# Combination and norm by tiles in one program, the attention half of the output projection first, a third modulation group in the preparation

## The chip, the cores and the metric

One Trainium2 chip; the kernel uses one core of it. The metric is the device time of one execution in microseconds (us). The engines are TensorE (PE; its weight loads are shown apart as PEld), VectorE (DVE), ScalarE (ACT), GpSimd (POOL) and SyncE (SP). Each runs its own stream of instructions in order and waits on semaphores. SP, ACT and POOL also issue the DMA transfers.

## The reference

The trunk of a diffusion backbone: 1024 latent and 256 context tokens of width 1024, two layers, everything in fp32.

```python
for layer in range(2):
    # six rows per condition: shift1, scale1, gate1, shift2, scale2, gate2
    mods = silu(cond) @ mod_w[layer] + mod_b[layer]      # cond: c (latent), c_ctx (context)
    h = rms_norm(x) * (1 + scale1) + shift1
    if layer == 0:                                       # [attention | RWKV-7] side by side
        u = h @ w_in
        a = gqa_attend(...)                              # 512 columns
        v, kk, w, k, r = rwkv_prepare(token_shift(u))    # sigmoids, exps, per-head norm of k
        y = delta_scan(forward) + delta_scan(backward)   # 512 columns
        y = group_norm(y) * gn_w + gn_b + sum(r * k * r_k) * v
        out = concat([a, y * g]) @ w_out                 # g = sigmoid(glr) @ g2
    else:
        out = differential_attention(h) @ w_out
    x = x + gate1 * out
    h = rms_norm(x) * (1 + scale2) + shift2
    gates, expert_id = top-1 group, then top-2 experts in it
    x = x + gate2 * sum_k gates[k] * expert_mlp(h)[k]    # 32 experts, sorted into blocks of rows
return rms_norm(x_latent) * final_gain
```

## The kernel before

The tokens are cut into ten tiles of 128 rows (`NT`); the first two (`CT`) are context. `build` (L3570) runs the phases one after another, each a block with one stream per engine, and a phase starts when the one before is complete on all engines. In the order of the first layer: modulation's first group (`mods_phase`), `norm_phase`, input projection, attention, `rwkv_shared_phase` (L1192), `rwkv_prep_phase` (L1296, "the preparation"), the scan, `readout_outproj_phase` (L2369, "the readout"), `route_phase` (L2958), `experts_phase`, `combine_phase` (L3444), and then the second layer's `norm_phase` ("n1"), which reads from DRAM what `combine_phase` wrote there.

**Modulation.** The product silu(cond) @ mod_w is cut into six groups of 2048 columns over both layers, each written as (layer, group). A group needs eight loads of 1 MB (`Mods.load`, on SP) into a ring of `MRING` = 4 slots, eight products of four matmuls each (`Mods.product`, L122), and one addition of the bias on DVE (`Mods.add`, L130). Load n waits until product n - 4 has been done. Two groups are in the shared and preparation phases ((0,2) and (1,0)) and two in the first layer's route phase ((1,1) and (1,2)); the results go to DRAM at the end of the phase. Groups of layer 1 are read by the second layer's phases.

**Preparation.** SP's stream loads the input rows, the small columns of the first head pair and the identity, then two modulation loads, then 52 small constants of the scan (`const.load_constants`, L1266 to L1282), then ten more modulation loads. ACT copies the transposed values (`vt`), squares the keys (`sq`), takes the roots of the head norms, then the sigmoids and exponentials of the decay. DVE multiplies and adds over 128 x 1281 elements from the normed key up to `key1` (L1475), adds the modulation groups, and makes `ksum`, `rk0` and `rk`. PE does modulation products 3 and 4, the transposes `vt`, product 5, the head norms `n0` to `n2`, the low-rank products, products 6 to 15, and last the ten `srk` matmuls (L1401), which wait for `rk`. The scan starts when this is done.

**Readout.** Rounds m of two row tiles u. DVE's `read(m)` centres and norms y (L2629 is its first instruction, a sum over each head), POOL makes the bonus and the weighing and copies the gate operand `gs` (L2486), PE makes the gates (`bankG`, L2522), and DVE multiplies them to `yo`. `yo` is written to DRAM beside the attention's half and read back as one row `o` of 1024. PE turns `o` (L2532), ACT copies the turned tile to fp32r (`oh`, the lead) and DVE subtracts it from the original (`ol`, the rest); the weights are split in the same way into `wh` (ACT, L2600) and `wl` (DVE, L2674), out of a ring of two loads. `products` (L2543) are 24 matmuls for each half of 512 columns: lead times lead, lead times rest and rest times lead for eight rows k. `RowNorm` (L2247) norms the result tile, turns it and computes the router's logits (L2361). In the stream of every engine, round 0, the weights and round 1 stand ahead of the loop over tiles.

**Route.** PE does four modulation products (loads with a ring of 4) before the matmul that ranks the tokens, two and four between the steps, and the rest after the matmuls that make the list of slots; DVE copies the list (L3240) and adds the two groups. The stage ends when the groups are in DRAM.

**Combination.** Pairs of tiles: POOL gathers the two experts' rows of each token (indirect DMAs), DVE scales and adds them, multiplies with gate2 (L3528) and adds x; ACT stores the result (L3559). After that n1 loads it again, norms it and turns it into the resident `hT` (lead and rest), which the second layer's projection (first load at L695) reads.

## Time and profile before

| | |
|---|---|
| timed runs | 4481.32, 4473.69, 4473.89 us; median 4473.89 |
| the profiled execution's own time | 4474.47 us |
| its span in the trace | 4472.7 us |
| mean granted clock of PE (share of full speed) | 0.917 |
| busy PE / PEld | 3745.6 us (84%) / 2428.8 us (54%) |
| busy DVE / ACT / POOL | 1867.3 (42%) / 1373.7 (31%) / 576.5 us (13%) |

The shares are means over many phases. In the trace the preparation lies between 744.78 and 848.91 us, the scan up to about 1606, the readout between 1606.19 and 1839.82, the route phase up to 1911.84, and combination and n1 together between 2601.20 and 2725.17. The granted clock is given as a share of 2.4 GHz: 0.50 is 1.2 GHz.

In rows of the timeline the first number is the start in us from the span's start, the second the time in us to the end of the group; then engine (SPq and ACTq are the queues' own instructions), line, operation, output <- inputs, shape, and how many instructions stand together. Brackets give the idle time before it and what ended it.

### The profile page before, as it was taken

How to read it: one execution, taken by the hardware profiler on the slowest of the kernel's cores; microseconds unless marked ns; L12 is line 12 of the kernel's file. 1: busy time of each engine (PE TensorE's matmuls, PEld its weight loads, DVE VectorE, ACT ScalarE, POOL GpSimd, SP SyncE). 2: the span in 40 equal slices, each digit the busy share in tenths (PEclk: the TensorE clock that was granted, in tenths of full speed). 3: DMA queues.
4: the chain of work that ended last, by engine and by line, in shares of the span. 5: the costliest groups of instructions: out<-in, count | busy, mean ns of one | idle time of the engine just before them, and what ended most of it. 6: DMA issues, size and time to landing. Idle time of an engine off the chain costs nothing. (4 is left out here: it accounts for less than half of the span.)

```text
span 4472.7 us, 88140 instructions
## 1 busy us (share of the span) xinstructions
PE 3745.6 (84%) x34494; PEld 2428.8 (54%) x34495; DVE 1867.3 (42%) x4520; ACT 1373.7 (31%) x3101; POOL 576.5 (13%) x898
## 2 busy tenths in 40 slices
PE   3998996698988959679999926998999795999992
PEld 1886553488888837423333305896666582333331
DVE  3322554677777656400000045424777653000004
ACT  2211564366666322011111102113666520111111
POOL 0000000034444323000000020100000010000001
PEclk6999998799999979689999967999999896999996
DMA  6221002422222244489997883214000234899984
GB/s 247 71 86 73 10 10 79 151 60 79 68 78 73 58 133 156 166 350 364 389 375 311 323 312 108 86 65 156 10 11 10 89 123 181 340 360 400 412 355 178
DMA packets 250474, 772.07 MB, mean 173 GB/s; under 512 B 76624, under 2 KB 164688, under 8 KB 219056
## 3 DMA queue, kind: packets, MB, share of 16 engines
q1 hardware_dynamic: 200624, 646.00, 38.6%
q10 hardware_dynamic: 36144, 72.89, 4.3%
q0 software_dynamic: 13392, 48.76, 2.8%
q8 instruction: 225, 3.69, 0.4%
q14 instruction: 89, 0.73, 0.1%
HBM read 642.16 MB, written 117.54 MB: 170 GB/s over the span
## 5 line engine op out<-in xcount | busy, mean ns | idle before, releaser
L3372 PE MATMUL ex_bY<-ex_w,ex_aT 128*64 x880 | 390.8, 597 | 51.0 <-DVE ex_aT L3437 46.2
L3372 PE MATMUL ex_bG<-ex_w,ex_xT 128*64 x880 | 392.3, 599 | 17.3 <-DMA ex_w<-in_moe_w_gate 17.3
L3372 PE MATMUL ex_bU<-ex_w,ex_xT 128*64 x880 | 390.5, 597 | 7.6 <-DMA ex_w<-in_moe_w_up 7.6
L3373 PE MATMUL ex_bG<-ex_w,ex_xT 128*64 128x512 f32 x880 | 392.3, 599 | 0.0
L3373 PE MATMUL ex_bY<-ex_w,ex_aT 128*64 128x512 f32 x880 | 391.1, 597 | 0.0
L3373 PE MATMUL ex_bU<-ex_w,ex_xT 128*64 128x512 f32 x880 | 390.5, 597 | 0.0
L3435 DVE TENSOR_TENSOR ex_a<-ex_sg,ex_bU 128x512 f32<-128x512 f32 x55 | 37.9, 689 | 771.8 <-PE ex_bU L3373 771.8
L3372 PEld LDWEIGHTS ex_bY<-ex_w,ex_aT 128*64 128x64 f32 x880 | 116.4, 137 | 278.5 <-issue 278.5
L3372 PEld LDWEIGHTS ex_bG<-ex_w,ex_xT 128*64 128x64 f32 x880 | 121.6, 139 | 268.4 <-issue 268.4
L3372 PEld LDWEIGHTS ex_bU<-ex_w,ex_xT 128*64 128x64 f32 x880 | 121.2, 138 | 258.0 <-issue 258.0
L1037 DVE TENSOR_SCALAR_CACHE_REDUCE ad_p<-ad_S 128x512 f32<-128x512 f32 (+1 forms) x384 | 215.6, 600 | 100.0 <-PE ad_S L947 100.0
L3408 ACT ACTIVATE ex_xT<-ex_tr 128x512 f32<-128x512 f32 x114 | 62.1, 595 | 509.4 <-PE ex_tr L3362 509.4
L3441 DVE COPY ex_y<-ex_bY 128x512 f32<-128x512 f32 x55 | 38.1, 692 | 409.9 <-PE ex_bY L3373 409.9
L947 PE MATMUL ad_S<-ad_K,ad_q 64*128 64x512 f32 (+1 forms) x768 | 191.4, 577 | 17.8 <-DMA ad_lqk<-in_od_lk 12.7
L973 PE MATMUL ad_acc<-ad_V,ad_pT 128*128 128x128 f32 x1280 | 187.8, 286 | 17.8 <-ACT ad_pT L1118 17.8
L485 PE MATMUL p_acc<-hT,p_wh 128*128 128x512 f32 (+1 forms) x480 | 175.9, 366 | 16.4 <-DVE p_wl L500 16.4
L973 PEld LDWEIGHTS ad_acc<-ad_V,ad_pT 128*128 128x128 f32 x1280 | 158.2, 192 | 53.6 <-ACT ad_pT L1118 33.4
L1086 ACT ACTIVATE ad_p<-ad_p,ad_nmax 128x1280 f32<-128x1280 f32 x128 | 173.5, 1355 | 6.0 <-DVE ad_nmax L1042 6.0
L485 PE MATMUL p_acc<-hT_rest,p_wh 128*128 128x512 f32 (+1 forms) x480 | 173.7, 362 | 0.0
L1037 DVE TENSOR_SCALAR_CACHE_REDUCE al_p<-al_S,rq 128x512 f32<-128x512 f32 (+1 forms) x208 | 126.3, 646 | 113.4 <-PE al_S L947 112.5
L485 PE MATMUL p_acc<-hT,p_wl 128*128 128x512 f32 (+1 forms) x480 | 173.2, 361 | 0.0
L1892 PE MATMUL rs_bankZ<-rs_X,rs_Bm 64*64 64x64 f32 x2560 | 137.2, 225 | 42.0 <-DVE rs_Bm L2178 29.1
(493 smaller groups left out, 8596.4 us busy)
## 6 DMA issues: line engine op xcount, KB each, us to landing
ex_w<-in_moe_w_gate SPq DMA_DIRECT2D x65, 2048.0 KB, 11.7
ex_w<-in_moe_w_up SPq DMA_DIRECT2D x65, 2048.0 KB, 14.8
ex_w<-in_moe_w_down SPq DMA_DIRECT2D x65, 2048.0 KB
yb_dram<-ex_y ACTq DMA_DIRECT2D x55, 512.0 KB, 10.2
rm_mw<-in_mod_w SPq DMA_DIRECT2D x16, 1024.0 KB, 8.1
rt_mw<-in_mod_w SPq DMA_DIRECT2D x16, 1024.0 KB, 8.2
kb_dram<-rs_pout SPq DMA_DIRECT2D x60, 256.0 KB, 2.7
rs_KB<-kb_dram SPq DMA_DIRECT2D x120, 128.0 KB, 2.7
```

Of the source, the lines that this page charges most:

```text
L485: mm = nc.tensor.matmul(acc[u % 2][c][:, 0:n], a[:, u // 2, k, at], b[:, k, t0:t0 + n], start=k == 0 and x == 0, stop=k == KT - 1 and x == 2)
L947: x = nc.tensor.matmul(S[j % 2][c][:, 0:w], q[h, pair, t * P - q_from:(t + 1) * P - q_from], K[h, kmap(pair), a:a + w], start=True, stop=True)
L973: x = nc.tensor.matmul(acc[m % 2][:, 0:VW], pT[:, g % 3, k * P:(k + 1) * P], V[:, kt, vc:vc + VW], start=kt == 0, stop=kt == nk - 1)
L1037: nc.vector.tensor_scalar(p[:, u, c, a:a + w], S[j % 2][c][:, 0:w], scale, None, ALU.mult, ALU.max, accum_out=top[:, u, c, i:i + 1]).then_ ...
L1086: nc.scalar.activation(p[:, u, c, 0:W], p[:, u, c, 0:W], ACT.Exp, bias=nmax[:, u, c:c + 1], accum_out=total[:, u, c:c + 1]).then_inc(p_don ...
L1892: x = nc.tensor.matmul(out[hp], left[hp], right[hp], start=start, stop=stop)
L3372: nc.tensor.matmul(bank[0:BR, :], stationary[:, k, 0:BR], w[:, ds(slot + (offset + k * n), 512)], start=k == 0, stop=k == total - 1)
L3373: m = nc.tensor.matmul(bank[BR:P, :], stationary[:, k, BR:P], w[:, offset + k * n:offset + k * n + 512], start=k == 0, stop=k == total - 1)
L3408: nc.scalar.activation(xT[:, 4 * b:4 * b + 4, :], tr[b][:, :].rearrange("p (k t) -> p k t", k=4), ACT.Copy).then_inc(xT_done, 1)
L3435: nc.vector.tensor_tensor(a[:, :], sg[:, :], bU[:, :], ALU.mult).then_inc(a_done, 1)
L3441: nc.vector.tensor_copy(y[:, 512:1024], bY[1][:, :]).then_inc(ye_dve, 1)
```

## The change

Four edits.

1. **Modulation groups.** (1,1) moves from the route phase to the preparation, which now has three groups of eight in a ring of 5 (`PREP_RING`) in place of two in a ring of 4; the route phase keeps one group of eight. The third group's bank is `bank[3]`. The last six products stand behind `srk` in PE's stream, and the third `add` behind `const.columns` in DVE's. In SP's stream two modulation loads move ahead of the columns, and the 52 scan constants move to the head of ACT's stream.
2. **Readout.** The attention's half is loaded alone (`oa`) and `yo` stays in SBUF in a ring of four, so that its store and the reload of the whole row are gone. Weights have six places, made of `w`, `t` and the norm's `h`. Of round 0 the products with the first four rows of the weights (`LEAD`) are issued for both tiles first, and the others (`REST`) when `yo` is there. ACT's and DVE's streams have round 0 and the weights interleaved; the gates 2 to 4 stand behind the first tile's products in PE's stream.
3. **`combine_norm_phase`** is new and takes the place of `combine_phase` and `norm_phase` n1 between the layers: one loop over single tiles gathers, combines, norms and turns. The shift is added by a matmul of shift rows with a unit pattern, the turn is a matmul with the identity, both into one bank. `x2` is still stored, not read again.
4. `build` keeps the slots and gates of layer 0 open across the phases (`places`).

```diff
-FIRST_GROUPS, NORM_GROUPS, PREP_GROUPS, ROUTE_GROUPS = [(0, 0)], [(0, 1)], [(0, 2), (1, 0)], [(1, 1), (1, 2)]
-PREP_EARLY = 3
+FIRST_GROUPS, NORM_GROUPS, PREP_GROUPS, ROUTE_GROUPS = [(0, 0)], [(0, 1)], [(0, 2), (1, 0), (1, 1)], [(1, 2)]
+PREP_RING, PREP_EARLY = 5, 3
...
@@ rwkv_shared_phase, SP
-                for n in range(MRING):
+                for n in range(PREP_RING):
                     mods.load(sp, n)
                 mods.load_bias(sp)
@@ rwkv_prep_phase, SP
                     load_padded(sp, x[:, i, :], projT[A_COLS + c0:A_COLS + c0 + P, :], x_in)
+                for n in range(PREP_RING, PREP_RING + 2):
+                    mods.load(sp, n)
...
                 sp.dma_start(ind[:, :], d["headcols"]).then_inc(c_in, 16)
-                for n in range(MRING, MRING + 2):
-                    mods.load(sp, n)
-                const.load_constants(sp)
-                for n in range(MRING + 2, mods.n):
+                for n in range(PREP_RING + 2, mods.n):
                     mods.load(sp, n)
@@ PE
-                for n in range(PREP_EARLY, MRING + 1):
+                for n in range(PREP_EARLY, PREP_RING):
                     mods.product(pe, sil, n)
...
-                mods.product(pe, sil, MRING + 1)
+                mods.product(pe, sil, PREP_RING)
                 ac.wait(pe, "sq")
...
-                for n in range(MRING + 2, mods.n):
+                for n in range(PREP_RING + 1, mods.n - 6):
                     mods.product(pe, sil, n)
                 dv.wait(pe, "rk")
                 for t in range(NT):
                     mm = nc.tensor.matmul(bank[2][:, 2 * t:2 * t + 2], a[:, 1, gap(t * P):gap(t * P) + P], ind[:, :], start=True, stop=True)
                 pp.did("srk", mm)
+                for n in range(mods.n - 6, mods.n):
+                    mods.product(pe, sil, n)
@@ ACT
+                const.load_constants(act)
                 for b in range(3):
                     pp.wait(act, f"vt{b}")
@@ DVE
-                for g in range(len(PREP_GROUPS)):
+                for g in range(len(PREP_GROUPS) - 1):
                     mods.add(dve, g)
...
                 const.columns(dve)
+                mods.add(dve, len(PREP_GROUPS) - 1)
@@ readout_outproj_phase
+        oa, yo = s.sb("oa", [P, 2, AW]), s.sb("yo", [P, 4, BW])
...
+        w_at = [z[:, u, :] for z in (w, t, norm.h) for u in US]
+        LEAD, REST = range(4), range(4, KT)
@@ SP
                 load_y(0)
+                load_w(0)
+                load_o(0)
...
                 sp.dma_start(ident[:, :], d["ident"]).then_inc(c_in, 16)
+                for k in range(1, 6):
+                    load_w(k)
+                load_y(1)
+                for k in range(6, KT):
+                    load_w(k)
@@ PE
+                pe.wait_ge(c_in, 16)
+                for u in US:
+                    turn(0, u, 0)
                 gates(0)
                 gates(1)
...
+                for u in US:
+                    if u == 0:
+                        pe.wait_ge(w_rest, len(LEAD))
+                    lo[0].wait(pe, f"lo{u}", 0)
+                    for b in US:
+                        products(0, u, b, LEAD)
+                for u in US:
+                    turn(0, u, 1)
+                pe.wait_ge(w_rest, KT)
                 for q in range(NT + 2):
                     m, u = divmod(q, 2)
...
+                    if q == 0:
+                        for n in range(2, 5):
+                            gates(n)
@@ ACT
+                lead_weights(range(1))
+                squares(0)
+                lead_weights(range(1, 2))
+                roots(0)
+                lead_weights(range(2, 4))
+                for u in US:
+                    lead(0, u, 0)
                 for q in US:
                     lift_gate(q)
...
+                lead_weights(REST)
                 for u in US:
+                    lead(0, u, 1)
+                squares(1)
+                roots(1)
@@ DVE
+                centre(0)
+                rest_weights(range(1))
+                spread_of(0)
+                rest_weights(range(1, 2))
+                normal(0)
+                rest_weights(range(2, 4))
                 for u in US:
-                    rest(0, u)
+                    rest(0, u, (0,))
+                gated(0)
+                rest_weights(REST)
+                for u in US:
+                    rest(0, u, (1,))
                 read(1)
+                dve.wait_ge(gate_in, 32)
                 norm.prepare(dve)
```

The new phase, its waits for the reuse of buffers cut:

```python
# SP: gate rows, x tiles 0 and 1, ident, scale rows, shift rows; then by tiles load_x(q + 2), store x2(q)
# POOL: by tiles the index copy, then two indirect gathers, four slots
# PE
for q in range(NT):
    u = q % 2
    scaled.wait(pe, q)
    for b in range(2):
        for k in range(4):
            n = 4 * b + k
            to = tr[u][b][:, k * P:(k + 1) * P]
            nc.tensor.matmul(to, shift_rows[:, cond(q), :], unit[:, n, :], start=True, stop=False)
            z = nc.tensor.matmul(to, h[:, u, n * P:(n + 1) * P], ident[:, :], start=False, stop=True)
        turned.did(z)
# ACT
weigh(0)                                  # first = yr[0] * gates[0]
for q in range(NT):
    if q + 1 < NT:
        weigh(q + 1)
    if q:
        lift(q - 1)                       # waits turned(q-1, b), copies bank b to the lead, twice
    summed.wait(act, q)
    squared.did(nc.scalar.activation(junk[:, :], x[:, q % 4, :], ACT.Square, accum_out=ss[:, u:u + 1]))
    squared.wait(act, q)
    rooted.did(nc.scalar.activation(sd[:, u:u + 1], ss[:, u:u + 1], ACT.Sqrt, scale=1.0 / D, bias=eps[:, 0:1]))
lift(NT - 1)
# DVE
for q in range(NT):
    weighed.wait(dve, q)
    joined    # t = yr[1] * gates[1] + first
    gated     # t = t * gate2
    summed    # x = x + t
    if q:
        leave(q - 1)                      # rest = bank - lead, twice
    rooted.wait(dve, q)
    united    # reciprocal
    scaled    # h = x * rstd * (1 + scale1)
leave(NT - 1)
```

## Rows read from the trace of the kernel before

**Rows 1.** Windows: length, then busy us by engine, PEclk, DMA share, GB/s.

```profile
744.78:848.91 104.13, 47.02 (x188) 14.26 (x188) 65.25 (x63) 27.85 (x33) 7.49 (x13) 0.63 0.60 208
1606.19:1839.82 233.63, 177.89 (x820) 141.08 (x820) 123.40 (x181) 58.70 (x108) 74.28 (x50) 0.81 0.43 149
2601.20:2725.17 123.97, 19.61 (x80) 15.68 (x80) 84.69 (x104) 26.69 (x51) 29.28 (x30) 0.50 0.65 238
```

**Rows 2.** Timeline, SP's queue in the preparation: first and last of 52 issues.

```profile
781.36 0.66 SPq L1266 DMA_DIRECT2D pwl<-in_ev_w  x1
...
806.90 0.42 SPq L1282 DMA_DIRECT2D sfirst<-in_first  x1
```

**Rows 3.** Source view of L3559, issues on ACT: ns min/median/max, starts.

```profile
L3559 ACTq DMA_DIRECT2D x_dram<-cb_x x10: 338/338/359, 2623.6 to 2661.6; - x10
```

**Rows 4.** Timeline of the preparation.

```profile
769.67 1.38 POOL L1260 MEMSET pwl<- 128x1536 f32 x1
...
788.27 1.55 ACT L1409 ACTIVATE vtok<-rm_bank 128x512 f32<-128x512 f32 x3 [22.48 <-PE rm_bank L1381]
...
794.97 0.83 DVE L1445 TENSOR_SCALAR rp_x<-rp_x 128x1281 f32<-128x1281 f32 x1 [3.39 <-ACT rp_x L1416]
...
831.75 1.48 DVE L1475 TENSOR_TENSOR bk<-rp_restart,rp_cum 128x1281 f32<-128x1281 f32 x1
...
842.91 4.43 PE L1401 MATMUL rm_bank<-rp_ind,rp_a 128*128 128x2 f32 x20 [4.66 <-DVE rp_a L1482]
```

**Rows 5.** Timeline, PE, two modulation products in a row.

```profile
834.72 1.86 PE L122 MATMUL rm_bank<-rm_mw,sil 128*32 128x512 f32 x8 [0.56 <-DMA rm_mw<-in_mod_w]
...
837.18 1.06 PE L122 MATMUL rm_bank<-rm_mw,sil 128*32 128x512 f32 x8 [0.60 <-DMA rm_mw<-in_mod_w]
```

**Rows 6.** DMA issues of a load of 1 MB: count, KB each, median us to landing.

```profile
p_w<-in_od_w_in SPq DMA_DIRECT2D x12, 1024.0 KB, 5.2
```

**Rows 7.** Timeline of the route phase and the next stage's first issue.

```profile
1842.57 2.37 SPq L107 DMA_DIRECT2D rt_mbias<-in_mod_b  x8
...
1896.64 0.20 DVE L3240 CAST tok<-rt_bankT 128x37 uint32<-128x37 f32 x1 [4.71 <-PE rt_bankT L3052]
...
1908.07 0.69 DVE L130 TENSOR_TENSOR rt_mbias<-rt_macc,rt_mbias 128x512 f32<-128x512 f32 x1 [10.51 <-PE rt_macc L122]
...
1911.84 0.36 SPq L3286 DMA_DIRECT2D ex_ident<-in_ident  x1
```

**Rows 8.** Timeline of the readout.

```profile
1645.81 1.23 DVE L2674 TENSOR_TENSOR ro_wl<-ro_w,ro_wh 128x1024 fp32r<-128x1024 f32 x1 [1.54 <-ACT ro_wh L2600]
...
1652.00 1.27 DVE L2629 TENSOR_REDUCE ro_mean<-ro_yr 128x8 f32<-128x512 f32 x2
...
1661.97 1.42 PE L2543 MATMUL ro_acc<-ro_wh,ro_oh 128*128 128x512 f32 x1
...
1675.15 1.03 PE L2532 MATMUL ro_tr<-ro_ident,ro_o 128*128 128x128 f32 x8
...
1680.54 1.27 DVE L2629 TENSOR_REDUCE ro_mean<-ro_yr 128x8 f32<-128x512 f32 x2
...
1690.74 1.12 PE L2522 MATMUL ro_bankG<-ro_g,ro_gs 128*128 128x512 f32 x2 [1.90 <-POOL ro_gs L2486]
```

**Rows 9.** Timeline of combination and norm, and the next stage's first issue.

```profile
2614.13 0.17 DVE L3521 COPY cb_gt<-gates 128x2 f32<-128x2 f32 x1 [12.80 <-DMA cb_yr<-yb_dram,cb_idx]
...
2620.00 2.35 DVE L3528 TENSOR_TENSOR cb_t<-cb_t,cb_gate 128x1024 f32<-128x1024 f32 x2
...
2725.17 1.02 SPq L695 DMA_DIRECT2D p_w<-in_od_w_in  x2
```

**Rows 10.** Timeline of the readout's loop over tiles, norm and router.

```profile
1705.47 1.95 PE L2361 MATMUL ro_bankH<-ro_wr,ro_w 128*128 128x36 f32 x16
...
1707.38 1.07 ACT L2295 ACTIVATE ro_sq<-ro_x 128x1024 f32<-128x1024 f32 x1 [1.31 <-DVE ro_x L2669]
...
1709.09 1.28 DVE L2316 SCALAR_TENSOR_TENSOR ro_h<-ro_x,ro_nrstd,ro_scale_row 128x1024 f32<-128x1024 f32 x1
```

More of the change, by code:

```diff
@@ L2522, in gates @@
                     rp.did(f"g{u}", nc.tensor.matmul(bankG[:, :], gs[:, u, :], g2[:, :], start=True, stop=True))
-                def turn(m, u):
-                    pe.wait_ge(o_in[u], 16 * m + 16)
-                    for b in US:
-                        if u:
-                            lo.wait(pe, f"lo{b}0", m)
-                        elif m:
-                            lo.wait(pe, f"lo{b}1", m - 1)
-                        for k in range(4):
-                            z = nc.tensor.transpose(tr[b][:, k * P:(k + 1) * P], o[:, u, (4 * b + k) * P:(4 * b + k + 1) * P], ident[:, :])
-                        pt.did(f"T{b}{u}", z)
@@ L2535, in products, with turn @@
-                def products(m, u, b):
-                    if m == 0 and u == 0:
-                        pe.wait_ge(w_rest, KT)
-                    lo.wait(pe, f"lo1{u}", m)
-                    if m:
-                        dv.wait(pe, f"g{b}{u}", m - 1)
-                    for k in range(KT):
+                def turn(m, u, b):
+                    if b:
+                        rd.wait(pe, f"out{u}", m)
+                    else:
+                        pe.wait_ge(o_in[u], 16 * m + 16)
+                    if u:
+                        lo[b].wait(pe, "lo0", m)
+                    elif m:
+                        lo[b].wait(pe, "lo1", m - 1)
+                    for k in range(4):
+                        part = yo[:, (2 * m + u) % 4, k * P:(k + 1) * P] if b else oa[:, u, k * P:(k + 1) * P]
+                        z = nc.tensor.transpose(tr[b][:, k * P:(k + 1) * P], part, ident[:, :])
+                    pt[b].did(f"T{u}", z)
@@ L2542, in products @@
+                def products(m, u, b, ks):
+                    for k in ks:
                         for n, (p, q) in enumerate(((oh, wh), (oh, wl), (ol, wh))):
                             z = nc.tensor.matmul(acc[u][b][:, :], p[:, u, k, :], q[:, k, b * 512:(b + 1) * 512], start=k == 0 and n == 0, stop=k == KT - 1 and n == 2)
-                    pp.did(f"o{b}{u}", z)
+                    if ks[-1] == KT - 1:
+                        pp.did(f"o{b}{u}", z)
+                pe.wait_ge(c_in, 16)
@@ L2546, in _ @@
+                for u in US:
+                    turn(0, u, 0)
                 gates(0)
                 gates(1)
-                pe.wait_ge(c_in, 48)
                 for u in US:
-                    turn(0, u)
-                for q in range(2, 5):
-                    gates(q)
+                    if u == 0:
[3 more added lines that the diff above has]
+                        products(0, u, b, LEAD)
@@ L2556, in _ @@
                         for b in US:
-                            products(m, u, b)
+                            lo[1].wait(pe, f"lo{u}", m)
+                            if m:
+                                lo[0].wait(pe, f"lo{u}", m)
+                                dv.wait(pe, f"g{b}{u}", m - 1)
+                            products(m, u, b, range(KT) if m else REST)
+                    if q == 0:
+                        for n in range(2, 5):
+                            gates(n)
                     if q >= 2:
@@ L2571, in _, with squares @@
                 act.wait_ge(eps_set, 1)
-                def spreads(m):
+                def squares(m):
                     for u in US:
@@ L2619, in _ @@
                     if u == 0 and m + 2 < ROUNDS:
-                        spreads(m + 2)
+                        squares(m + 2)
+                        roots(m + 2)
             @block.vector
@@ L2650, in read, with rest_weights, rest @@
                         rd.wait(dve, f"add{u}", m)
[L2651 to L2657 removed]
+                        if m >= 2:
+                            pt[1].wait(dve, f"T{u}", m - 2)
+                        rd.did(f"out{u}", nc.vector.tensor_tensor(yo[:, (2 * m + u) % 4, :], yt[:, u, :], gated_in[:, u, :], ALU.mult))
+                def read(m):
+                    centre(m)
+                    spread_of(m)
+                    normal(m)
+                    gated(m)
+                def rest_weights(ks):
+                    for k in ks:
+                        dve.wait_ge(w_lead, k + 1)
+                        nc.vector.tensor_tensor(wl[:, k, :], w_at[k % 6], wh[:, k, :].bitcast(F32), ALU.subtract).then_inc(w_rest, 1)
+                def rest(m, u, bs):
+                    for b in bs:
+                        ac[b].wait(dve, f"T{u}", m)
                         at = (slice(None), u, slice(4 * b, 4 * b + 4), slice(None))
[L2659 removed]
+                        lo[b].did(f"lo{u}", nc.vector.tensor_tensor(ol[at], tr[b][:, :].rearrange("p (k t) -> p k t", k=4), oh[at].bitcast(F32), ALU.subtract))
                 def result(m, u):
@@ L3620, in build @@
                     bank = [s.ps(f"bank{i}") for i in range(8)]
-                    mods = Mods(nc, s, d, PREP_GROUPS, bank[6:8])
+                    mods = Mods(nc, s, d, PREP_GROUPS, [bank[6], bank[7], bank[3]], ring=PREP_RING)
                     rwkv_shared_phase(nc, sems, d, projT, lora, gate, mods, sil)
@@ L3637, in build @@
         odd_outproj_phase(nc, sems, d, o, x2, x3, h, L)
-        moe(1, x3, out, CT, d["final_gain"], L)
+        slots, gates = places(ctx, 1, NT - CT)
+        moe(1, CT, slots, gates, L)
+        combine_phase(nc, sems, "cb1", d, 1, yb, x3, out, slots, gates, CT, d["final_gain"])
+    routed.close()
 def shape_constants():
```

243 lines of the change are left out of this document (174 added, 69 removed).

## The prediction

> **What bounds the kernel now.** I read the profile by stage, since the change touches four that run one after another and nothing between them. The table of windows [rows 1] shows three of them: the preparation of the recurrence (104 us, VectorE (DVE) busy for 65), the readout with the output projection (234 us, TensorE (PE) busy for 178), and the combination with the norm behind it (124 us, PE busy for 20, at the half clock of 1.2 GHz throughout). The fourth is the first layer's route stage. Then I followed each stage's last wait.
>
> Preparation: ScalarE (ACT) starts `vt` at 788.27 and DVE continues at 794.97, after which DVE is nearly full until `key1` ends at 833.23 [rows 4]. Modulation products come at the pace of their loads, 2.46 us each [rows 5]; the last one holds DVE for 4.5 us, then `rk` releases the ten `srk` matmuls at 842.91 [rows 4]. Route: the list of slots is copied at 1896.64, but the stage goes on to 1911.84 for six more products and one `add` [rows 7]. Readout: the first products start at 1661.97; the DVE read of round 2 starts at 1680.54, and its gates release PE at 1690.74 [rows 8]. From there PE is the bound. Combination and norm: the first gathered tile is there at 2614.13, the next stage starts at 2725.17 [rows 9].
>
> **Preparation.** The change moves 52 constant DMAs (4 + 3 x 14 + 6) from SyncE's (SP) queue to the head of ACT's stream, before `vt`. On SP they take 781.36 to 807.32, 0.50 us each [rows 2]; they are hidden there, since only the modulation loads stand behind them. On ACT a single issue takes 0.34 [rows 3]. ACT can start them once the pwl clear is done, at 771.05 [rows 4]; at 0.50 each they end at 797.0. I take SP's price, because it is that of these very DMAs in a row; the bound below is 52 x 0.34, ending at 788.7. Behind them wait `vt`, `sq`, PE's norm matmuls, the square roots, and for those DVE. Thus: 797.0 + 1.55 for `vt` [rows 4] + 1.4 (`sq`) + 4.3 (norm matmuls; 2.4 before, but PE will have stood idle and be at 1.2 GHz) + 1.4 = 805.7 for the DVE row that was at 794.97, so 10.7 later. SP has two modulation loads earlier instead, which saves PE its wait, but nothing in this order uses that.
>
> From 794.97 to the end of `rk` were 47.9 us with 4.5 of waiting [rows 4]; without the wait, `rk` ends at 805.7 + 43.4 = 849.1. The first two groups' adds are ready by then. `srk` takes 4.4 [rows 4]: 853.5. Only now come the last six products. Ring 5 has loads 18 to 22 there; load 23 waits for product 18 (1.9 [rows 5]), lands 5.2 after issue [rows 6], and its product takes 1.9: 862.5. The add is 0.7, and the stores with the stage's end 3.1, as at the end of route [rows 7]: 866.3. The stage ended at 848.91 [rows 1]: **+17.4**. If ACT were not held at all, `rk` would end near 836 and the last products alone would bring the end to 853, +4. If every issue took 0.6 it would be +23. The extra load and four extra bias DMAs in the shared stage end on SP before ACT's sigmoid does: nothing.
>
> The Trainium skill ("DMA: Bandwidth & Descriptors", anatomy of one DMA) gives about 50 ns for a sequencer's dispatch on its software path and says that issuing from several engines saves only issue time. By 50 ns the 52 would cost ACT 2.6 us; the trace's SP rows say ten times that.
>
> **Route.** One group of 8 instead of two. The six late products are gone, and group (1,2) is complete long before the list. List copy ends at 1896.84; add 0.7; 3.1 to the next stage [rows 7]: 1900.6. Four bias DMAs less ahead of the weight loads (0.30 each [rows 7]) bring the first four products, behind which PE's rank matmul stands, 1.2 forward: 1899.4 against 1911.84, **-12.4** (-11 to -13.5).
>
> **Readout.** Weights no longer wait in a ring of two, and half of each product needs no readout. Before, weights were split by 1647.0 and only then did DVE read round 1 (1652.00) [rows 8]. Now DVE has read(0) up to `nrm` and four splits at 1.23 each [rows 8]; with loads at some 1.3 us each, I put the fourth split and the first `lo` at 1624. PE then does the attention half of tiles 0 and 1: 48 matmuls, as many as tile 0 took from 1661.97 to 1675.15, its slow start included: 13.2 [rows 8]. That ends at 1637.2; the turns, ACT's copies and DVE's `lo` for the other half take 5: read(1) starts at 1642.2, not 1652.0. It and the norm's preparation take 13.5, and the other 24 matmuls of tile 0 are done by about 1646, so DVE no longer waits for them: result(0), rest and scale take 6 more, and read(2) starts at 1661.7, not 1680.54: 18.8 earlier. PE's gates are behind that read by the same 10.2 us, as POOL (GpSimd) copies gs only after weighing [rows 8]. PE has a gap before it, which I charge with 2.5 of half clock. After that PE is the bound as before, with the same instructions; so **-16** remains, not more: the attention half leaves PE idle later. Bounds: -22 with no slow starts, -6 if loads, weights and POOL's contention delay the first half by ten. The removed store and reload of yo lay beside other work: nothing.
>
> **Combination with norm.** 124 us before [rows 1]. The new loop is serial: PE turns tile q-1 (T), ACT copies the second bank (0.6) *before* it squares tile q, then root, reciprocal and scale. Square to the end of scale is 1709.09 + 1.28 - 1707.38 = 3.0 [rows 10]. With handoffs the period is T + 3.8. DVE alone needs 6.7 and is not the bound. T: shift is now a matmul, and the turn is one as well instead of a transpose; each is two records in fp32, so 32 a tile. At 1.2 GHz a record costs 0.22 (20 in 4.43 [rows 4]), at 2.4 GHz 0.12 (16 in 1.95 [rows 10]): T is 7.1 or 3.9. With 7 us of matmuls in a row, the clock may rise on the way, as it did within tile 0's products [rows 8]; I take T = 6.1, period 9.9. The first tile: gathered and constants in at 2614.1 [rows 9], 3 for unit and scale rows, 3.8 for three operations at 1.2 to 1.3 (2.35 for two [rows 9]), 4.4 with the table load and scale: 2625.4. Nine periods: 2714.5; last turn and splits 7.6, stage end 0.8: 2722.9 against 2725.17 [rows 9], **-2**. Cold throughout: 2625.4 + 98 + 9.4 = 2732.8, +8. At the full clock: 2625.4 + 69.3 + 6.2 = 2700.9, -24.
>
> The Trainium skill ("TensorE: Matmul & The Clock Gate", the HAM clock gate) calls the half clock the default and sustained activity what lifts it; by it I would expect neither end but the middle, and tile 0's slow start agrees.
>
> **Sum:** 17.4 - 12.4 - 16 - 2 = -13. The profiled execution took 4474.5 (span 4472.7, so 1.8 around it), 0.6 above the median of the three timed runs: 4461.
>
> **Rivals.**
> 1. ACT is hardly held by its 52 issues: the preparation costs +4 instead of +17. For it: ACT's single issue was already shorter than SP's; against it: SP's row of 52. 4474 - 27 = 4447. Chance 0.13.
> 2. PE stays at 2.4 GHz in the new combination: -24 there, 4474 - 35 = 4439. Its busy share would be half, and this stretch had none of that clock before [rows 1]. Chance 0.13.
> 3. The readout's early half is given back: POOL and the reads set tile 2 as before, and only 0 is left of -16: +3, 4477. For it speaks the wait of PE for POOL at 1690.74 [rows 8]. Chance 0.16.
> 4. Slower: ACT's issues, beside SP's, wait for each other. At 0.9 us each ACT is free at 818, 21 us later than I said, and the kernel ends at 4482 to 4490. It turns to a loss at 0.75 each (25.96 + 13 over 52); SP's rows in that stretch are 0.66 and 0.42, mean 0.50 [rows 2]. Chance 0.12.
> Forecast as it stands: 0.46, from 4453 to 4469.
>
> **How the numbers follow.** About 0.2%, 9 us, is what a measurement of this kernel can tell from no change. Of the forecast 0.33 lies beyond that and 0.13 within. Faster: 0.33 + 0.13 + 0.13 = 0.59. Same: 0.13 + 0.16 = 0.29. Slower: 0.12. The range from 4437 to 4476 takes in rivals 1 and 2 and most of 3.
>
> **What would show it.** Right: ACT's first `vt` near 797 and a queue of 52 issues on ACT ahead of it; scan's first DMA near 866; the experts' first instruction 12 us sooner after route's start; read(2) some 55 us after the readout's start, against 74; in the new stage tiles 9 to 11 us apart, ACT's square waiting behind its copy of bank 1. Wrong: `vt` before 790, tiles under 8.5 us apart, or read(2) over 65 us after the start.

## The result and the profile after

The changed kernel took 4529.69 us (median of four runs, 4526.65 to 4534.46) against 4475.4 for the kernel before: 1.0122 times as long, 95% interval 1.011 to 1.0135. The forecast was 4461, in a range up to 4476. The profiled execution took 4526.65 with a span of 4524.6, 51.9 more than before.

The windows of the changed kernel by stage, with the columns of [rows 1]: preparation, readout, route, and the new phase.

```profile
743.61:874.25 130.64, 53.96 (x252) 17.87 (x252) 65.85 (x64) 27.73 (x33) 7.91 (x13) 0.66 0.68 230
1629.63:1848.95 219.32, 171.42 (x820) 136.79 (x820) 127.55 (x181) 58.42 (x108) 74.96 (x50) 0.86 0.38 134
1848.95:1910.55 61.60, 27.01 (x134) 13.41 (x134) 35.77 (x140) 1.79 (x3) 0.52 (x1) 0.56 0.36 142
2598.76:2776.80 178.04, 116.41 (x320) 79.84 (x320) 66.74 (x73) 37.25 (x61) 22.92 (x30) 0.50 0.37 130
```

Beside [rows 1] the four stretches read: preparation +26.5 (130.64 against 104.13), readout -14.3 (219.32 against 233.63), route -10.4 (61.60 against the 72.02 between 1839.82 and 1911.84 [rows 7]), combination with norm +54.1 (178.04 against 123.97). The shared stage began 1.2 earlier and scan and experts were 3 shorter together: 51.6, of the 51.9. So one stage is off the forecast by far. Its window shows PE busy for 116 us where it was 20 before, all at the half clock.

**The new phase.** Its timeline over one tile, with the columns of the timelines above:

```profile
2639.88 1.29 DVE L3768 SCALAR_TENSOR_TENSOR cn_h<-cn_x,cn_rstd,cn_scale_row 128x1024 f32<-128x1024 f32 x1
...
2641.22 0.79 PE L3698 MATMUL cn_tr<-cn_unit,cn_shift_rows 8*128 8x128 f32 x2 [3.57 <-DVE cn_h L3768]
2641.94 0.50 PEld L3699 LDWEIGHTS cn_tr<-cn_ident,cn_h 128*128 128x128 f32 x2 [0.22 <-issue]
2641.94 0.80 PE L3699 MATMUL cn_tr<-cn_ident,cn_h 128*128 128x128 f32 x2
...
2642.67 0.50 PEld L3698 LDWEIGHTS cn_tr<-cn_unit,cn_shift_rows 8*128 8x128 f32 x2 [0.23 <-issue]
...
2652.90 0.60 ACT L3713 ACTIVATE hT<-cn_tr 128x512 fp32r<-128x512 f32 x1 [5.19 <-PE cn_tr L3699]
2653.39 1.05 ACT L3728 ACTIVATE cn_junk<-cn_x 128x1024 f32<-128x1024 f32 x1
...
2654.89 0.16 DVE L3764 RECIPROCAL cn_rstd<-cn_sd 128x1 f32<-128x1 f32 x1 [0.67 <-ACT cn_sd L3730]
2655.09 1.28 DVE L3768 SCALAR_TENSOR_TENSOR cn_h<-cn_x,cn_rstd,cn_scale_row 128x1024 f32<-128x1024 f32 x1
...
2656.43 0.79 PE L3698 MATMUL cn_tr<-cn_unit,cn_shift_rows 8*128 8x128 f32 x2 [3.57 <-DVE cn_h L3768]
```

The loop is the serial one of the forecast: scale, turn, ACT's copy of the second bank, square, root, reciprocal, scale. Its period is 15.2 us (2641.22 to 2656.43), and PE stands idle for only 3.57 of it. Each pair of records, one matmul, takes 0.72 (2641.22, 2641.94, 2642.67), and between two pairs no weight load runs for 0.22. Sixteen such matmuls are 11.6, where I had put 6.1, and 7.1 as the bound.

**Preparation.** The timeline up to the scan's first DMA:

```profile
770.16 0.75 ACTq L1267 DMA_DIRECT2D pwl<-in_ev_w  x1
...
789.40 2.77 ACTq L1279 DMA_DIRECT2D pmu<-in_ev_mu_prev  x1
...
804.95 0.45 ACTq L1283 DMA_DIRECT2D sfirst<-in_first  x1
805.45 1.36 ACT L1412 ACTIVATE vtok<-rm_bank 128x512 f32<-128x512 f32 x3 [40.57 <-issue]
...
814.18 0.83 DVE L1448 TENSOR_SCALAR rp_x<-rp_x 128x1281 f32<-128x1281 f32 x1 [21.35 <-ACT rp_x L1419]
...
857.54 4.43 PE L1401 MATMUL rm_bank<-rp_ind,rp_a 128*128 128x2 f32 x20 [10.59 <-DVE rp_a L1485]
...
874.25 0.71 SPq L1813 DMA_DIRECT2D rs_KB<-kr  x1
```

The 52 issues held ACT from 770.16 to 805.45, 0.68 each. The DVE row that answers to 794.97 of [rows 4] stands at 814.18; from there everything follows at the forecast distances.

**Readout and route.** The timeline: the last two of the first four weight splits, first product, the reads of rounds 1 and 2, the gates behind them; then the copy of the list.

```profile
1646.80 4.48 DVE L2703 TENSOR_TENSOR ro_wl<-ro_t,ro_wh 128x1024 fp32r<-128x1024 f32 x2
...
1656.65 1.42 PE L2545 MATMUL ro_acc<-ro_wh,ro_oh 128*128 128x512 f32 x1
...
1673.98 1.27 DVE L2662 TENSOR_REDUCE ro_mean<-ro_yr 128x8 f32<-128x512 f32 x2
...
1694.04 1.27 DVE L2662 TENSOR_REDUCE ro_mean<-ro_yr 128x8 f32<-128x512 f32 x2
...
1704.17 2.07 PE L2526 MATMUL ro_bankG<-ro_g,ro_gs 128*128 128x512 f32 x2 [11.16 <-POOL ro_gs L2490]
...
1906.53 0.20 DVE L3296 CAST tok<-rt_bankT 128x37 uint32<-128x37 f32 x1 [4.70 <-PE rt_bankT L3108]
...
1910.55 0.36 SPq L3342 DMA_DIRECT2D ex_ident<-in_ident  x1
```

From the stage's start the first product is at 27.0 instead of 55.8 [rows 8], read(1) at 44.4 instead of 45.8, read(2) at 64.4 instead of 74.4, the gates at 74.5 instead of 84.6.

### The profile page after: what moved, and what is told of

It reads as the page before. It is cut to its first block and busy times, and to the rows that moved or that the text cites. A ratio compares the mean times of both kernels' runs of the same rounds, so it can differ in the third digit from the quotient of the medians.

```text
span 4524.6 us, 88425 instructions
## 1 busy us (share of the span) xinstructions
PE 3827.1 (85%) x34734; PEld 2485.7 (55%) x34735; DVE 1852.8 (41%) x4489; ACT 1382.3 (31%) x3111; POOL 570.1 (13%) x898
## 5 line engine op out<-in xcount | busy, mean ns | idle before, releaser
L3428 PEld LDWEIGHTS ex_bU<-ex_w,ex_xT 128*64 128x64 f32 x880 | 121.7, 139 | 258.6 <-issue 258.6
L974 PE MATMUL ad_acc<-ad_V,ad_pT 128*128 128x128 f32 x1280 | 186.9, 285 | 17.8 <-ACT ad_pT L1119 17.8
## 6 DMA issues: line engine op xcount, KB each, us to landing
yb_dram<-ex_y ACTq DMA_DIRECT2D x55, 512.0 KB, 10.4
```

What stands on the lines that cost most here:

```text
L974: x = nc.tensor.matmul(acc[m % 2][:, 0:VW], pT[:, g % 3, k * P:(k + 1) * P], V[:, kt, vc:vc + VW], start=kt == 0, stop=kt == nk - 1)
L3428: nc.tensor.matmul(bank[0:BR, :], stationary[:, k, 0:BR], w[:, ds(slot + (offset + k * n), 512)], start=k == 0, stop=k == total - 1)
```

## The experiments

Each is the changed kernel with one edit, if nothing else is said; ratios are to the kernel before. "Stretch" is the window of the new phase (178.04 in the changed kernel).

**Where the loss lies.** The old phases back in place:

```diff
-        combine_norm_phase(nc, sems, d, yb, x1, x2, slots, gates, hT)
+        combine_phase(nc, sems, "cb0", d, 0, yb, x1, x2, slots, gates, 0, None)
+        norm_phase(nc, sems, "n1", d, 1, SHIFT1, x2, hT, d["ident"])
```

> The changed kernel with the separate combination and norm of the kernel before in place of the new phase; all else as changed. Theory A (the loss lies wholly in the new phase): its stretch was 178.0 us against 124.0, so this kernel comes to 4529.7 - 54 = 4475.7, the same as before: preparation +26.5, readout -14.3, route -10.4, small ones -4 cancel. Rival B (part of the loss is an effect that the phase tally hides, such as later phases that start colder or the slots kept open): it stays above 4485.

4475.9 us, ratio 1.000 (0.9991 to 1.001), stretch 125.98. The other three edits cancel out; the loss is the new phase.

**What the turn costs.** The shift matmul left out, the other with `start=True`:

> The changed kernel without the eight shift matmuls of each tile (the shift row is left out of the computation). Theory A (PE's turn stands in the serial period, each fp32 matmul of 128 columns costs 0.72 at the half clock, whatever its rows): turn 5.8 instead of 11.6, period 15.2 - 5.8 = 9.4, the stretch 178 - 58 = 120, kernel 4472. Rival B (the order of ACT and DVE or the gathers set the period, PE's turn is mostly hidden): less than 20 us gained, period above 13. Rival C (a matmul with 8 rows is cheap and the turn by identity dear): less than 20 us too, but with matmul records of the identity alone longer than 0.5.

The timeline of its PE in one tile:

```profile
2638.91 3.49 PEld L3698 LDWEIGHTS cn_tr<-cn_ident,cn_h 128*128 128x128 f32 x16 [3.86 <-DVE cn_h L3767]
2638.91 3.78 PE L3698 MATMUL cn_tr<-cn_ident,cn_h 128*128 128x128 f32 x16 [3.57 <-DVE cn_h L3767]
```

The stretch fell by 78 us to 99.71, more than the 58 of theory A, and the period to 7.35 (2638.91 to 2646.26). The eight remaining matmuls take 3.5, which is 0.44 each and not 0.72, at the same half clock. Removing half of the matmuls made the other half cheaper. (The kernel's time, 4414.04, can't be compared: with other values in the second layer its router fills fewer blocks, and the gate matmul of that layer's experts has 400 records instead of 432.) This set a new question: why a record costs 0.36 in the changed kernel and 0.22 here.

**Transposes, the shift on DVE:**

```diff
-                            nc.tensor.matmul(to, shift_rows[:, cond(q), :], unit[:, n, :], start=True, stop=False)
-                            z = nc.tensor.matmul(to, h[:, u, n * P:(n + 1) * P], ident[:, :], start=False, stop=True)
+                            z = nc.tensor.transpose(to, h[:, u, n * P:(n + 1) * P], ident[:, :])
...
+                    shifted.did(V.tensor_tensor(h[:, u, :], h[:, u, :], shift_row[:, cond(q), :], ALU.add))
```

> The changed kernel with eight transposes for each tile instead of sixteen matmuls, and the shift added by one VectorE instruction of 1.22 us, as in the norm before. Theory A: PE needs 2.0 a tile (the row of the norm before), the serial chain by PE would be 6.8, and DVE becomes the bound: 3.75 to the sum, 1.7 for square and root, 0.2 + 1.3 + 1.2 = 8.1 a tile; the stretch 28 + 9 x 8.1 + 4 = 105, kernel 4529.7 - 73 = 4457. Rival B (gathers at some 6.4 us a tile and their latency set the pace once PE is short): period above 10, kernel above 4474.

4460.41, ratio 0.9965 (0.9951 to 0.9979), stretch 109.23. Theory A holds within 4 us (stretch 105, kernel 4457): joining the two phases is a gain of 15 us if the turn is cheap.

**The order of ACT and DVE.** ACT's `lift(q - 1)` behind the root of tile q, DVE's `leave(q - 1)` behind the scaling of tile q:

> The changed kernel with ACT's copies of tile q-1 behind square and root of tile q, and DVE's rests of tile q-1 behind the scaling of tile q; the matmuls stay. Theory A: the chain is opened, PE goes from tile to tile without a gap, the period is its own 11.6 and the stretch 28 + 10 x 11.6 + 3 = 147, kernel 4498. If PE, without gaps, is granted the full clock, the period falls to some 6 to 8 and the kernel to 4460. Rival B (another wait, of the buffers of h or of the banks, takes the place): period stays near 15, kernel near 4529.

Its window of the phase:

```profile
2603.42:2749.63 146.21, 115.78 (x320) 79.85 (x320) 65.87 (x73) 37.35 (x61) 22.93 (x30) 0.50 0.45 159
```

4497.64, ratio 1.0052 (1.0035 to 1.0069), stretch 146.21 against 147 forecast. Here PE works without gaps for 116 us of the window, and is still granted half the clock.

**What makes the alternation dear.** The same sixteen matmuls, first the four shifts of a bank, then the four turns:

```diff
-                            nc.tensor.matmul(to, shift_rows[:, cond(q), :], unit[:, n, :], start=True, stop=False)
-                            z = nc.tensor.matmul(to, h[:, u, n * P:(n + 1) * P], ident[:, :], start=False, stop=True)
+                            nc.tensor.matmul(tr[u][b][:, k * P:(k + 1) * P], shift_rows[:, cond(q), :], unit[:, n, :], start=k == 0, stop=False)
+                        for k in range(4):
+                            n = 4 * b + k
+                            z = nc.tensor.matmul(tr[u][b][:, k * P:(k + 1) * P], h[:, u, n * P:(n + 1) * P], ident[:, :], start=False, stop=k == 3)
```

> The changed kernel with the same sixteen matmuls for each tile in another order: in each bank first the four shift matmuls (8 rows), then the four by the identity (128 rows), as one accumulation. In the kernel without shift a record took 0.22 us, in the changed kernel 0.36; so something in the alternation costs 0.14 a record, 4.5 a tile. Theory M (alternating weights of 8 and 128 rows keeps the next weight load from running beside the matmul): the turn falls from 11.6 to about 7.1, the period to 10.7, the stretch from 178 to 133, kernel 4485. Rival N (the second matmul writes on the same 128 columns right behind the first and waits for it): here the writes are four matmuls apart, so the same numbers. Rival O (accumulating with start=False is itself slow in fp32, or 0.36 is just the price in this stretch): little change, the stretch above 165.

The timeline of its PE:

```profile
2649.55 2.07 PE L3697 MATMUL cn_tr<-cn_unit,cn_shift_rows 8*128 8x128 f32 x8 [3.57 <-DVE cn_h L3769]
2651.55 1.78 PEld L3700 LDWEIGHTS cn_tr<-cn_ident,cn_h 128*128 128x128 f32 x8 [0.22 <-issue]
2651.55 2.08 PE L3700 MATMUL cn_tr<-cn_ident,cn_h 128*128 128x128 f32 x8
2653.56 1.78 PEld L3697 LDWEIGHTS cn_tr<-cn_unit,cn_shift_rows 8*128 8x128 f32 x8 [0.22 <-issue]
```

4491.58, stretch 142.98. Inside a group a weight load takes 0.22 and follows the one before without a gap (1.78 for 8); the gap of 0.22 without a weight load is still there, but only where the height (the number of rows of the weights) changes, at each of the four groups of a tile and not at each of sixteen matmuls. The turn is therefore 8.1 and not the 7.1 of theory M, which is why the stretch is 10 us above its 133. Rival O is out. N is not yet.

The alternation kept, but the shift's operands 128 rows high, rows 8 to 127 zero:

```diff
-        ident, unit = s.sb("ident", [P, P]), s.sb("unit", [KT, KT, P])
-        gate, scale_row, shift_rows = s.sb("gate", [P, 2, D]), s.sb("scale_row", [P, 2, D]), s.sb("shift_rows", [KT, 2, P])
+        ident, unit = s.sb("ident", [P, P]), s.sb("unit", [P, KT, P])
+        gate, scale_row, shift_rows = s.sb("gate", [P, 2, D]), s.sb("scale_row", [P, 2, D]), s.sb("shift_rows", [P, 2, P])
...
+                V.memset(shift_rows[:, :, :], 0.0).then_inc(unit_set, 1)
```

> The changed kernel with the shift's operands made 128 rows high (rows 8 to 127 of both are zero), the alternation of the sixteen matmuls kept. Theory M (heights): all weights now have 128 rows, a record falls to 0.22, the stretch to 133, kernel 4485. Rival N (same columns in a row): nothing changes, the stretch near 178, kernel 4530. Rival O: nothing changes either.

The timeline of its PE, two matmuls at the full clock, then at the half clock:

```profile
2636.44 0.39 PE L3699 MATMUL cn_tr<-cn_unit,cn_shift_rows 128*128 128x128 f32 x2
2636.66 0.39 PE L3700 MATMUL cn_tr<-cn_ident,cn_h 128*128 128x128 f32 x2
...
2645.30 0.55 PEld L3700 LDWEIGHTS cn_tr<-cn_ident,cn_h 128*128 128x128 f32 x2
...
2645.73 0.55 PEld L3699 LDWEIGHTS cn_tr<-cn_unit,cn_shift_rows 128*128 128x128 f32 x2
```

and its window:

```profile
2599.59:2725.56 125.97, 64.44 (x320) 62.57 (x320) 66.94 (x74) 37.26 (x61) 22.97 (x30) 0.65 0.51 184
```

4477.99, ratio 1.0015, stretch 125.97. More rows made it faster by 52 us. One matmul now starts every 0.43 (2645.30, 2645.73), accumulation and columns being the same as in the changed kernel: theory M. The clock also rises for part of each tile (mean 0.65), so that the turn takes 6.4 on average and the stretch stays under theory M's 133. The same price of a change comes out of two arrangements: an alternating matmul takes 0.72 against 0.43 here, 0.29 more, and a group of eight records takes 2.00 from start to start (2649.55, 2651.55) where eight at this pace are 1.72, 0.28 more.

The Trainium skill ("TensorEngine Tiling (Array Packing)", Key Properties) says that changing the tiling mode, and not just the tile, drains TensorE, and "TensorE: Matmul & The Clock Gate" (LDWEIGHTS) that a load's time goes by its columns and not its rows. The runs agree with the second: eight loads of 8 rows and eight of 128 rows take the same 1.78. They fit the first, since each change of height adds a gap; that 8 rows count as a mode of their own is my reading, which no run here shows by itself.

**Shift ahead of the wait**, one matmul of 512 columns for a bank, issued before `scaled.wait`:

```diff
-                    scaled.wait(pe, q)
...
+                        nc.tensor.matmul(tr[u][b][:, :], shift_rows[:, cond(q), :], unit[:, 4 * b:4 * b + 4, :].rearrange("j k t -> j (k t)"), start=True, stop=False)
+                    scaled.wait(pe, q)
```

> The changed kernel with the shift of a bank as one matmul of 512 columns, issued before the wait for the scaled tile, and the eight matmuls by the identity behind it. Theory A with M or N: behind the wait only 16 records of 0.22 remain, 3.5 us, and the two shift matmuls (about 1.6 each) lie in PE's gap of 3.6; period 7.4 as without the shift, the stretch 28 + 67 + 5 = 100, kernel 4529.7 - 78 = 4452. Rival O: the turn stays at 16 x 0.36 = 5.8, period 9.4, the stretch 120, kernel 4472.

The timeline of its PE, turn, the next tile's shift, turn:

```profile
2647.83 3.79 PE L3699 MATMUL cn_tr<-cn_ident,cn_h 128*128 128x128 f32 x16 [1.66 <-DVE cn_h L3768]
...
2651.54 3.78 PE L3694 MATMUL cn_tr<-cn_unit,cn_shift_rows 8*128 8x512 f32 x4
...
2655.25 3.78 PE L3699 MATMUL cn_tr<-cn_ident,cn_h 128*128 128x128 f32 x16
```

4448.69, ratio 0.9943 (0.9926 to 0.996), stretch 97.94, period 7.42, where theory A had 4452, 100 and 7.4. In the rows shown turn and shift, 3.71 each, fill the period without a gap.

**The clock.** Matmuls that nobody reads, of 512 columns, in PE's gap:

> The changed kernel with idle matmuls of 512 fp32 columns (identity by a constant, into a bank that nobody reads): eight ahead of the first tile and two in the gap ahead of each other one, some 3.1 us at the half clock in a gap of 3.6. Theory P (the half clock of the stretch comes from PE's gaps): the granted clock goes to full speed, the turn to some 6 to 8 us, the period to 10 or less, the stretch to 140 or less, kernel below 4492. Rival Q (matmuls of 128 columns with a weight load each don't raise the clock, and the wide ones in the gap are too few): the clock stays at half in most of the stretch, the stretch is as long or some us longer.

The timeline of its PE in one of the spans at the full clock:

```profile
2634.78 0.48 PE L3701 MATMUL cn_tr<-cn_unit,cn_shift_rows 8*128 8x128 f32 x2
2635.19 0.49 PE L3702 MATMUL cn_tr<-cn_ident,cn_h 128*128 128x128 f32 x2
```

4516.92, ratio 1.0092, stretch 162.77, mean clock 0.58. Neither theory as written: the full clock came in seven short spans, in which a matmul, two records, took 0.42 instead of 0.72, and was lost again in between. So alternation costs at the full clock too (0.42 against the 0.22 of equal heights). But its price at the half clock is what made the turn 11.6: a whole turn at the full clock would be 16 x 0.42 = 6.7 by these rows (an estimate), close to the 6.9 of equal heights at the half clock. So either the full clock or equal heights would have brought the turn near the forecast; the full clock was not reached for a whole tile in any of these runs.

**The preparation.** The constants on SP again, behind load 6:

> The changed kernel with the 52 constant loads back on SP, behind modulation load 6; three groups as changed. Theory A (ACT's issues hold up the whole preparation): ACT's first copy near 792, DVE's norm row near 798, but now the modulation loads come later again, product 17 near 843, srk to 849, the last load waits for product 18, and the stage ends near 862 instead of 874.3: kernel 4529.7 - 12 = 4517.5. Rival B (what held the stage is the third group and the order of loads, not ACT): end within 3 us of 874, kernel 4527 or more.

The timeline of its preparation, the turn for `vt` and the norm row:

```profile
785.37 2.40 PE L1382 MATMUL rm_bank<-rp_ident,rp_o 128*128 128x128 f32 x10 [17.04 <-DMA rp_ind<-in_headcols]
...
793.50 0.83 DVE L1448 TENSOR_SCALAR rp_x<-rp_x 128x1281 f32<-128x1281 f32 x1 [3.12 <-ACT rp_x L1419]
```

4519.85, ratio 1.0093; the scan's first DMA at 860.46 (theory A 862), 13.1 more than before from the stage's start.

The kernel before, with `const.load_constants` moved from SP to the head of ACT's stream and nothing else:

> The kernel before with one edit: the 52 constant loads at the head of ACT's stream. Theory A (each issue on ACT costs the 0.68 us seen in the changed kernel, 35 us in all): ACT's first copy near 806, DVE's norm row 20 us later than before, of which 4.5 are given back by a wait that goes, the stage +16, kernel 4491. Rival B (0.68 was the price of contention with SP's longer list there; alone an issue takes 0.34 to 0.50): ACT free by 789 to 797, the stage +0 to +6, kernel 4475 to 4481.

The timeline of its preparation:

```profile
771.35 0.73 ACTq L1266 DMA_DIRECT2D pwl<-in_ev_w  x1
...
806.82 0.45 ACTq L1282 DMA_DIRECT2D sfirst<-in_first  x1
...
816.05 0.83 DVE L1445 TENSOR_SCALAR rp_x<-rp_x 128x1281 f32<-128x1281 f32 x1 [21.94 <-ACT rp_x L1416]
...
859.42 4.43 PE L1400 MATMUL rm_bank<-rp_ind,rp_a 128*128 128x2 f32 x20 [12.23 <-DVE rp_a L1482]
```

4489.87, ratio 1.0033 (1.0022 to 1.0045). That is 13 us slower (theory A 4491). Fifty-two issues again take 35.9 us, without the third group, and `srk` stands 16.5 later than in [rows 4].

The constants on POOL, behind its clear:

> The changed kernel with the 52 constant loads on POOL, behind its clear, instead of ACT. Theory A (only ACT's time matters and POOL has nothing else to do): ACT's first copy near 792, DVE's norm row near 798, srk near 842, last product near 854, stage end near 859, 15 us earlier than in the changed kernel: 4514.5. Rival B (POOL's issues are dear, over 1 us each, and the constants come after DVE needs them at about 842): the end is set by them, and the gain is under 8 us.

The timeline of its preparation:

```profile
792.47 2.40 PE L1382 MATMUL rm_bank<-rp_ident,rp_o 128*128 128x128 f32 x10 [22.72 <-DMA rp_ind<-in_headcols]
...
793.62 0.60 ACT L1412 ACTIVATE vtok<-rm_bank 128x512 f32<-128x512 f32 x1 [28.31 <-PE rm_bank L1382]
...
800.59 0.83 DVE L1448 TENSOR_SCALAR rp_x<-rp_x 128x1281 f32<-128x1281 f32 x1 [6.44 <-ACT rp_x L1419]
...
800.70 0.84 POOL L1283 DMA_DIRECT2D sfirst<-in_first  x1
...
843.95 4.43 PE L1402 MATMUL rm_bank<-rp_ind,rp_a 128*128 128x2 f32 x20 [8.99 <-DVE rp_a L1485]
...
860.85 0.71 SPq L1813 DMA_DIRECT2D rs_KB<-kr  x1
```

4517.14, ratio 1.0086. An issue takes 0.59 there. It holds no stream of compute, but it is not free: SP's own columns, issued beside it, reach PE 7.1 us later than in the run with the constants on SP (792.47 against 785.37), and the norm row is as much later. `srk` comes at 843.95, near the 842.91 of before, only because DVE has no modulation product left to wait for. The stage still ends at 860.85 (theory A 859), 13.7 more than before from its start, behind the six products, load 23, the add and the store.

**The readout.** The 48 products of the attention half of both tiles moved behind the other half's turn, in PE's stream alone:

> The changed kernel with the products of the attention half of tiles 0 and 1 moved behind the turn of the other half and the last weights in PE's stream; nothing else. Theory A (these 48 matmuls, 13.3 us, then stand between the turn and tile 0's rest, and gates 2 to 4 behind them, for which the reading of round 1 waits): the readout becomes 8 to 10 us longer, kernel 4538 to 4540, that is most of the 14 us that the readout had gained. Rival B (the gain came from the interleaved weights and the shorter way of yo, and PE's gap of 11 us ahead of gate 5 takes the products in): under 3 us longer.

4537.62, ratio 1.0133; readout 226.46 against 219.32, 7.1 more (theory A 8 to 10), read(2) 7.4 later. Half of the 14.3 us is the early products; how the other half is shared between weights, reads and the shorter way of `yo`, no run separates.

**Two versions together.** Both have the shift ahead; one has the third group in the preparation and the constants on POOL, the other the preparation and route of the kernel before.

> The changed kernel with the shift ahead (one matmul of 512 columns a bank before the wait) and the constants on POOL. The two gains lie in phases apart: 80 us in the combination stretch and 12.8 in the preparation: 4529.7 - 80 - 13 = 4437. Against the kernel before: preparation +13.7, readout -14.3, route -10.4, combination -26.

> The changed kernel with the shift ahead, and the preparation and route phases of the kernel before (two modulation groups in each, ring of 4, constants on SP). Theory A (even with ACT free the third group costs the preparation 13.7 us, since its last six products, the last load and the store stand behind srk, and route gives back 10.4 only): 3 us faster than the run with POOL, about 4434. Rival B (the third group is a gain once ACT is free, and phases after the preparation profit from it): 3 us or more slower than that run.

4436.54, ratio 0.9909 (0.9891 to 0.9926), and 4432.84, ratio 0.9899 (0.9882 to 0.9915). By their traces preparation and route together are 178.8 against 175.3, and the kernels are 3.7 apart (theory A 3). The second is the fastest kernel of the study, 1.0% under the kernel before; in it the group isn't moved.

## Why the prediction was wrong

**The term that failed** is the combination's, "each is two records in fp32, so 32 a tile. At 1.2 GHz a record costs 0.22 (20 in 4.43)". Forecast -2 with bounds of +8 and -24, measured +54.1. A record cost 0.36. I read the price from `srk`, twenty records of one kind, and applied it to a row of matmuls whose weights alternate between 8 and 128 rows. Bound and value both rested on it, so the range couldn't hold the result. The rest of that step was right: handoffs of 3.6 (forecast 3.8), the chain through ACT's second copy, ten serial periods. With T = 11.6 for 6.1 the nine periods give 9 x 5.3 = 48, the last turn 5.5 more, the first tile was 2.9 later: 56, the difference between -2 and +54. With heights made equal the records cost what I had put, the turn took 6.4, the period was 10.0 (forecast 9.9), and the stretch 125.97, 4 from my 121.7: the forecast was that of another kernel. It should have had a row with mixed heights, or, as none was there, a bound from above that says so.

**The clock** was taken to rise on the way (6.1 between 7.1 and 3.9). In the changed kernel it never did, over 178 us with PE busy for two thirds, nor in the run with PE busy for 116 of 146. It did for a part of each tile in the run with equal heights, and in seven short spans in the run with wide matmuls in the gap. Of the 5.5 us by which a turn was longer, this term is 1 (7.1 for 6.1) and the alternation 4.5. What raises the clock in one and not in the other is not settled: the grouped run (0.50) and the run with transposes (0.50) did not get it either.

**Preparation**, +17.4 forecast, +26.5 measured. The term mis-sized is 52 x 0.50: it was 52 x 0.68. All that follows was right: vt to the norm row 8.7 (8.7), norm row to `srk` 43.4 (43.4), `srk` to the scan 16.7 (17.2). It is what rival 4 named, dearer issues on ACT, short of the 0.75 at which they alone would have decided. Why an issue costs 0.68 is not settled. The first 18, beside SP's small issues, took 0.77 each, the other 34 0.63; most rows are 0.45, a few 2 to 3 us. SP's issues grew dearer as well: in the kernel before its 26 for the columns took 12.5 us, with the constants on ACT as the only edit 13.8. So issues grew dearer on both sides; whether that is all of ACT's price, no run says. The Trainium skill ("Perfetto Trace Analysis", DMA Instruction — HWDGE) says that the sequencers share the block that makes descriptors, and that an issue's time holds the wait for its lock. The slower first 18 and SP's 26 agree; no run here shows the lock itself.

**Readout**, -16 forecast, -14.3 measured, but by two errors. The first products came at 27.0 and not 17.8 after the start, and read(2) at 64.4 and not 55.5, as DVE ended the fourth split only 21.6 after the start (1651.28 by the trace; 17.8 with the first `lo` forecast) and gates 0 and 1, which need POOL and ACT, stand ahead of the products in PE's stream. The last three of the four splits took 2.2 to 2.3 each, where I had used the 1.23 of [rows 8]; POOL was busy beside them, as it was beside the first two splits of the kernel before (4.26 together, the six later ones with POOL idle 1.22 to 1.23 each); that POOL is the reason no run tests. Against that, from the gates to the end took 144.8 us instead of 149.1, where I had said nothing changes. The windows of that part, before and after, have the same 680 matmul records:

```profile
1690.74:1839.82 149.08, 138.26 (x680) 114.06 (x680) 73.14 (x113) 35.66 (x71) 41.01 (x24) 0.90 0.39 134
1704.17:1848.95 144.78, 134.73 (x680) 111.11 (x680) 73.32 (x113) 36.17 (x71) 41.04 (x24) 0.92 0.31 110
```

So no work was gone from it: PE was busy 3.5 us less for the same records, at a mean granted clock of 0.92 instead of 0.90. The run with the early products moved back has 144.5 there as well. That gain was luck.

**Route**, -12.4 forecast, -10.4 measured: from the copy of the list to the next stage 4.0 (forecast 4.0), but the copy was 57.6 us after the start instead of 56.8; the four bias DMAs less brought nothing.

**The rivals.** Rival 2 (full clock) and rival 3 (readout given back) were not so, rival 1 (ACT hardly held) is refuted by the kernel before with ACT's 52 issues alone. Its price was low too: 794.97 + 43.4 is 838.4 and not 836, which with the forecast's own tail is +7 and not +4, and with the constants off ACT the stage took 13.1 and 13.7 more. None of the four named the cost of alternation, and the chance of slower, 0.12, rested on ACT alone.

## What to carry to other kernels

Take a matmul's price from a row with the same neighbours, not only the same shape: two kinds that alternate can cost more than both apart. Operands padded with zeros to the same height or one wide matmul ahead of the wait gave that back here, and grouping most of it. A stream's head is not a free place for small DMAs: count the issues and multiply by a row of that engine. When work moves from a stage to another, compare what both ends wait for; the third group cost 13 us where it went (117.0 against 104.2 in the last two kernels) and saved 9 where it left (61.8 against 71.1).

## What the runs showed of the hardware

- fp32 matmuls of 128 columns at the half clock: 0.22 us a record with weights of one height, 0.36 when 8 and 128 rows alternate; at the full clock 0.11 and 0.21. Each change of height leaves 0.22 without a weight load at the half clock and costs 0.28 to 0.29, alternating or grouped.
- A shift of 8 rows padded to 128 made the kernel 52 us faster.
- PE busy for 116 us without a gap in alternating matmuls was granted 1.2 GHz throughout; in the run with equal heights, with gaps between the tiles, the mean was 0.65 of full speed.
- A small DMA's issue: 0.68 on ACT, 0.50 on SP, 0.59 on POOL, each over the same 52. Issued from POOL beside SP's own, they brought SP's columns to PE 7.1 us later than issued behind them on SP.
